# Two-layer hybrid encoder with a routed expert layer: expert weights read in 8 KB runs, and eight bias products spread over TensorE's row groups

## What is computed

```python
mod = cond @ ada_w[layer] + ada_b[layer]                 # 6 x 1024: shift, scale, gate, twice
h = _modulate(_rmsnorm(x, norm_mix_g[layer]), sh_m, sc_m)
m = mixer(h)              # layer 0: window attention + RG-LRU; layer 1: S5 state space + GLU
x = x + g_m * m
h = _modulate(_rmsnorm(x, norm_ffn_g[layer]), sh_f, sc_f)
x = x + g_f * _hier_moe(h, ...)
# _hier_moe: each token picks one of 4 groups, then the top 2 of its 4 experts;
#   for every expert e:  he = silu(t @ w1[e]) * (t @ w3[e]);  out += gate * (he @ w2[e])
#   w1, w3: [1024, 512], w2: [512, 1024], 16 experts in each layer
# GLU of layer 1: zg = act @ glu_w + glu_b;  zg[:, :1024] * sigmoid(zg[:, 1024:])
```

## Time and profile before

| | us |
|---|---|
| median of 3 runs | 899.51 (896.71 to 900.66) |
| the profiled execution | 902.16 |
| its span in the trace | 900.4 |
| PE (matmul) busy | 831.8 (92%) |
| VectorE, ScalarE, GpSimd busy | 316.3, 199.7, 146.9 |
| mean granted TensorE clock | 0.971 |
| DMA, mean over the span | 317 GB/s, 285.33 MB |

### The profile page before, as it was taken

One profiled execution on the slowest core, in us unless ns is written; L12 is line 12 of the kernel. 1 busy time (PEld: TensorE's weight loads), 2 busy tenths in 40 slices (PEclk: granted clock), 3 DMA queues, 4 the chain that ended last, 5 costly groups with the idle time before them and its releaser, 6 DMA issues.

```text
span 900.4 us, 12803 instructions
## 1 busy us (share of the span) xinstructions
PE 831.8 (92%) x5243; PEld 452.6 (50%) x5244; DVE 316.3 (35%) x718; ACT 199.7 (22%) x329; POOL 146.9 (16%) x234
## 2 busy tenths in 40 slices
PE   3899989899999998999599999689999899999994
PEld 0477634565564653644456544434444554655641
DVE  1447993741230411311799410621000311312304
ACT  2402330521311312312500110511001212213112
POOL 2328678049000000000033100000000000000000
PEclk9999989999999999999789999989999999999997
DMA  9999999969999999997996892206877399999992
GB/s 323 334 377 386 353 393 270 371 247 397 387 397 397 391 393 397 392 392 286 396 349 223 323 325 93 95 1 235 312 235 249 102 394 395 392 398 391 395 399 92
DMA packets 126289, 285.33 MB, mean 317 GB/s; under 512 B 7092, under 2 KB 8388, under 8 KB 125992
## 3 DMA queue, kind: packets, MB, share of 16 engines
q1 hardware_dynamic: 123552, 277.88, 84.1%
q0 software_dynamic: 1984, 5.21, 1.9%
q10 hardware_dynamic: 712, 1.67, 0.5%
HBM read 279.50 MB, written 5.24 MB: 316 GB/s over the span
## 4 chain that ended last, share of the span: by engine, by line
PE 71%; DMA 10%; DVE 8%; SPq 8%; issue 1%; ACT 1%; DVEq 0%; ACTq 0%
PE PS L1665 15%; PE PS L1684 11%; PE PS L1692 8%; DMA ring<-in_moe_w 7%; SPq L355 6%; PE PS L1971 6%; PE PS L1668 6%; PE PS L1708 6%; PE PS L1623 3%; PE PS L1434 3%; PE PS L1404 3%; DMA ring<-in_ab_w_in 2%; PE PS L1489 2%; PE PS L1956 2%; PE PS L1506 2%; SPq L364 2%
## 5 line engine op out<-in xcount | busy, mean ns | idle before, releaser
L1684 PE MATMUL PS<-ring,work 128*64 128x512 f32 (+1 forms) x512 | 129.0, 595 | 0.8 <-DMA ring<-in_moe_w 0.8
L1665 PE MATMUL PS<-ring,hT 128*64 128x256 f32 x896 | 107.6, 382 | 7.6 <-DMA ring<-in_moe_w 7.5
L1665 PE MATMUL PS<-ring,yg 128*64 128x256 f32 x896 | 106.2, 379 | 0.0
L1279 DVE TENSOR_TENSOR work<-work,PS 128x512 f32<-128x512 f32 x32 | 22.0, 688 | 207.9 <-PE PS L1665 159.6
L1665 PEld LDWEIGHTS PS<-ring,hT 128*64 128x64 f32 x896 | 61.9, 137 | 50.2 <-DMA ring<-in_moe_w 11.0
L1684 PEld LDWEIGHTS PS<-ring,work 128*64 128x64 f32 (+1 forms) x512 | 42.7, 143 | 76.1 <-issue 70.8
L1665 PEld LDWEIGHTS PS<-ring,yg 128*64 128x64 f32 x896 | 64.4, 137 | 32.3
L1692 PE MATMUL PS<-work,xhat 128*128 128x256 f32 (+1 forms) x256 | 68.1, 426 | 7.5 <-issue 7.2
L1283 DVE COPY yg<-PS 128x512 f32<-128x512 f32 x32 | 22.1, 692 | 146.3 <-PE PS L1684 146.3
L1708 PE MATMUL PS<-yg,grow 64*128 64x512 f32 (+1 forms) x256 | 68.0, 606 | 0.0
L1692 PEld LDWEIGHTS PS<-work,xhat 128*128 128x128 f32 x256 | 50.1, 198 | 28.2 <-issue 21.9
(11 more groups left out here) (366 smaller groups left out, 974.9 us busy)
## 6 DMA issues: line engine op xcount, KB each, us to landing
ring<-in_moe_w SPq DMA_DIRECT2D x96, 2048.0 KB, 19.2
ring<-in_ada_w SPq DMA_DIRECT2D x20, 2048.0 KB, 15.9
work<-in_ada_w SPq DMA_DIRECT2D x4, 2048.0 KB, 14.4
ring<-in_s_glu_w SPq DMA_DIRECT2D x4, 2048.0 KB, 17.2
ring<-in_ab_w_in SPq DMA_DIRECT2D x3, 2048.0 KB, 25.3
ring<-in_ab_w_out SPq DMA_DIRECT2D x2, 2048.0 KB, 14.8
ring<-rot_tables SPq DMA_DIRECT2D x2, 2048.0 KB, 10.6
rot_tables<-grow POOLq DMA_DIRECT2D x8, 256.0 KB, 5.8
```

What stands on the lines that cost most here:

```text
L1279: v.tensor_tensor(he[:, e % 2, :], he[:, e % 2, :], bank[1], ALU.mult).then_inc(S("he_ready"), 1)
L1665: last = mm(dst[64 * u:64 * u + 64, 0:256], hg[k][:, e * P:e * P + 64], w[:, k, 256 * u:256 * u + 256], start=k == 0, stop=k == KD - 1)
L1684: last = mm(dst, left[:, at:at + (64 if narrow else P)], w[:, c4, h * HALF:(h + 1) * HALF], start=c4 == 0, stop=c4 == KF - 1)
```

## The change

Three things change.

1. The expert weights are laid out so that one partition holds four consecutive rows of w1 and w3 (two of w2) in HBM: `"l e (h p c) f -> l p e h (c f)"`. A run is then 8 KB for all three. The contraction index k = 4h + c now stands for the model columns h*512 + p*4 + c. So everything that meets these weights has to have the columns in that order: `norm` writes `xhat` of the expert layers through `quads` (a read with a stride of four elements, a contiguous write), silu and the gated product go through `pairs` (a read of PSUM with a stride of two), and scale and shift of the expert layers come from new columns `mod4` and `gain4`, filled by 4 more transposes (`row4`), three more copies on ScalarE, and in `ada_cols(1)` and `ada_cols(2)` four more small products each, with one more addition on VectorE. The router weights are loaded in that order too, by 8 instead of 4 transfers on GpSimd's queue. ScalarE's queue issues four transfers for `row4` and drops two for the old rows.
2. `glub` stands four times, on partitions 0, 32, 64 and 96. Its transfers move from ScalarE's queue (one) to GpSimd's (four), behind the wait `x_new >= 2`.
3. `glu_bias(m, part, q)` uses row group q. The two of pair 0 stand in row groups 0 and 1; the two of pair 1 are issued together in the last turn of the loop; the four of pairs 2 and 3 are issued together at m == 2. The wait for `grow_ready >= 3` moves there from m == 3.

```diff
-        w1_v = a["moe_w1"].rearrange("l e (k p) f -> l p e k f", p=P)
-        w3_v = a["moe_w3"].rearrange("l e (k p) f -> l p e k f", p=P)
-        w2_v = a["moe_w2"].rearrange("l e (k p) n -> l p e k n", p=P)
+        w1_v = a["moe_w1"].rearrange("l e (h p c) f -> l p e h (c f)", h=2, c=4)
+        w3_v = a["moe_w3"].rearrange("l e (h p c) f -> l p e h (c f)", h=2, c=4)
+        w2_v = a["moe_w2"].rearrange("l e (u p c) n -> l p e u (c n)", u=2, c=2)
...
-                sp_.dma_start(u3(MOE_BASE[L] + j, D if w == "w2" else FF), moe_src(L, w, group * EPG + e)).then_inc(
+                sp_.dma_start(u3(MOE_BASE[L] + j, SLOT // 2), moe_src(L, w, group * EPG + e)).then_inc(
...
+        quads = lambda ap: ap.rearrange("q (h p c) -> q h c p", h=2, c=4)
+        quads_out = lambda ap: ap.rearrange("q (h c p) -> q h c p", h=2, c=4)
+        pairs = lambda ap: ap.rearrange("q (u p c) -> q u c p", u=2, c=2)
+        pairs_out = lambda ap: ap.rearrange("q (u c p) -> q u c p", u=2, c=2)
...
-                    s.activation(xhat[:, 0, :], x[:, 0, :], ACT.Copy, scale=stat[:, 6:7]).then_inc(S("xhat0_ready"), 1)
+                    src, dst = x[:, 0, :], xhat[:, 0, :]
+                    if n % 2:
+                        src, dst = quads(src), quads_out(dst)
+                    s.activation(dst, src, ACT.Copy, scale=stat[:, 6:7]).then_inc(S("xhat0_ready"), 1)
...
-                        s.activation(he[:, e % 2, :], bank[0], ACT.Silu).then_inc(S("sil_ready"), 1)
+                        s.activation(pairs_out(he[:, e % 2, :]), pairs(bank[0]), ACT.Silu).then_inc(S("sil_ready"), 1)
...
-                        v.tensor_tensor(he[:, e % 2, :], he[:, e % 2, :], bank[1], ALU.mult).then_inc(S("he_ready"), 1)
+                        v.tensor_tensor(pairs_out(he[:, e % 2, :]), pairs_out(he[:, e % 2, :]), pairs(bank[1]), ALU.mult).then_inc(S("he_ready"), 1)
...
                 dve.wait_ge(S("ada_cols_ps"), i + 1)
+                if i:
+                    dve.wait_ge(S("cols_ready"), 2)
+                    m4 = by_c(mod4[:, i - 1, :, :].rearrange("p s k -> p (s k)"))
+                    v.tensor_tensor(m4, bank[7][:, P:P + 16].rearrange("p (c m) -> p c m", c=4), m4, ALU.add)
...
                     last = mm(bank[6 if i == 0 else 7][:, c4 * n:(c4 + 1) * n], arows[i][:, c4 * P:(c4 + 1) * P],
                               sel[:, r:r + n], start=True, stop=True)
+                if i:
+                    f = r + 2
+                    for c in range(4):
+                        last = mm(bank[7][:, P + 4 * c:P + 4 * c + 4], arows[i][:, c::4], sel[:, f:f + 4], start=True,
+                                  stop=True)
...
+            for c in range(4):
+                tr(bank[5][:, P + 12 * c:P + 12 * c + 12], row4[:, c::4], 12)
...
+            pool.wait_ge(S("x_new"), 2)
+            for q in range(4):
+                pool.dma_start(glub[q], a["s5_glu_b"][0].rearrange("(r n) -> r n", r=4)).then_inc(S("glub_in"), 16)
...
-            def glu_bias(m, part):
+            def glu_bias(m, part, q):
-                r = GLU_PAIRS[m][0] + 2 * part
-                mm(bank[GLU_BANK[m][part]], bcol(ident[0:4, r:r + 1]), glub, start=True, stop=False)
+                r = 32 * q + GLU_PAIRS[m][0] + 2 * part
+                mm(bank[GLU_BANK[m][part]], bcol(ident[32 * q:32 * q + 4, r:r + 1]), glub[q], start=True, stop=False)
...
-                    glu_bias(0, 0)
-                    glu_bias(0, 1)
+                    glu_bias(0, 0, 0)
+                    glu_bias(0, 1, 1)
...
-                    glu_bias(1, 0)
+                    glu_bias(1, 0, 0)
+                    glu_bias(1, 1, 1)
                     glu_blocks(1, 0, 0, 3)
...
             for m in range(1, 4):
-                if m == 3:
+                if m == 2:
                     pe.wait_ge(S("grow_ready"), 3)
+                    for q in range(4):
+                        glu_bias(2 + q // 2, q % 2, q)
                 for part in range(1 if m == 1 else 0, 2):
-                    glu_bias(m, part)
                     glu_blocks(m, part, 0, KD)
```

More of the change, by code:

```diff
@@ L77 @@
 _at = 0
-for _name, _n in (("mix0", KD), ("ffn0", KD), ("mix1", KD), ("ffn1", KD), ("s5d", KD),
+for _name, _n in (("mix0", KD), ("mix1", KD), ("s5d", KD),
                   ("conv_w", CONV * LT), ("conv_b", LT), ("ga_b", LT), ("gx_b", LT), ("lam", LT)):
@@ L272, in build @@
         actT = yg[:, 2:4, :].rearrange("p a (k t) -> p (a k) t", t=T)
-        glub = yg[0:4, 1, HALF:D]
+        glub = [yg[32 * q:32 * q + 4, 1, HALF:D] for q in range(4)]
         arow1 = yg[:, 1, 0:HALF]
@@ L479, in _ @@
             for L in range(2):
[L480 to L483, removed]
+                for h in range(2):
+                    at = slice(4 * h, 4 * h + 4)
+                    rows4 = slice(h * HALF, (h + 1) * HALF)
+                    pool.dma_start(wr_sb[:, L, at, 0:NG], a["moe_wg"][L, rows4].rearrange(
+                        "(p c) g -> p c g", c=4)).then_inc(S("small_in"), 16)
+                    pool.dma_start(wr_sb[:, L, at, NG:], a["moe_we"][L, rows4].rearrange(
+                        "(p c) g e -> p c (g e)", c=4)).then_inc(S("small_in"), 16)
                 pool.dma_start(rb[:, L, 0:NG], a["moe_bg"][L:L + 1].to_broadcast([P, NG])).then_inc(S("small_in"), 16)
@@ L657, in modulate @@
                     act.wait_ge(S("xT_ps"), 4 * n + k // 2 + 1)
-                    s.activation(hT[:, k, :], bank[k // 2][:, (k % 2) * T:(k % 2 + 1) * T], ACT.Identity, scale=modA[:, n, k:k + 1],
-                                 bias=mod[:, L, sec, k:k + 1]).then_inc(S("hT_act"), 1)
+                    scale, shift = scaling(n, k)
+                    s.activation(hT[:, k, :], bank[k // 2][:, (k % 2) * T:(k % 2 + 1) * T], ACT.Identity, scale=scale,
+                                 bias=shift).then_inc(S("hT_act"), 1)
             def gate_row(n):
@@ L675, in _ @@
                 S("cols_ready"), 1)
+            row4_t = bank[5][:, P:P + 48].rearrange("p (c n) -> p c n", c=4)
+            s.activation(by_c(mod4[:, :, :, :].rearrange("p l s k -> p (l s k)")), row4_t[:, :, 0:8], ACT.Copy)
+            for L in range(2):
+                last = s.activation(by_c(gain4[L]), row4_t[:, :, 8 + 2 * L:10 + 2 * L], ACT.Copy)
+            last.then_inc(S("cols_ready"), 1)
             def rows_out(i):
@@ L798, in hg_evac @@
                 def hg_evac(k, at):
-                    return s.activation(hg[k], bank[at], ACT.Identity, scale=modA[:, n, k:k + 1],
-                                        bias=mod[:, L, SH_F, k:k + 1])
+                    scale, shift = scaling(n, k)
+                    return s.activation(hg[k], bank[at], ACT.Identity, scale=scale, bias=shift)
                 pt = lambda m: pickT[:, 2 * m:2 * m + 2, :].rearrange("p e t -> p (e t)")
@@ L849, in ffn @@
                         act.wait_ge(S(f"over_used{L}"), SLOTS + 3 * e + 1)
-                        s.activation(he[:, 0, :], bank[0], ACT.Silu).then_inc(did, 1)
+                        s.activation(pairs_out(he[:, 0, :]), pairs(bank[0]), ACT.Silu).then_inc(did, 1)
                         act.wait_ge(pe_did, KD + 1 + e + 1)
@@ L953, in norm @@
                 if n < 4:
[L954 removed]
+                    src, dst = x[:, 1, :], xhat[:, 1, :]
+                    if n % 2:
+                        src, dst = quads(src), quads_out(dst)
+                    v.tensor_scalar(dst, src, stat[:, 7:8], None, ALU.mult).then_inc(S("xhat1_ready"), 1)
                 else:
@@ L974, in mod_scale @@
             def mod_scale(n):
[L975 to L978, removed]
+                L = n // 2
+                if n % 2:
+                    dst, src, gain = mod4[:, L, 1, :], mod4[:, L, 1, :], gain4[L]
+                else:
+                    at = ROWS[("mix0", "mix1")[L]][0]
+                    dst, src, gain = modA[:, L, :], mod[:, L, SC_M, :], cols[:, at:at + KD]
+                v.scalar_tensor_tensor(dst, src, 1.0, gain, ALU.add, ALU.mult).then_inc(S("modA_ready"), 1)
                 dve.wait_ge(S("modA_ready"), n + 1)
             def modulate(n):
-                L, sec = n // 2, (SH_M if n % 2 == 0 else SH_F)
                 for k in (2, 3, 6, 7):
                     dve.wait_ge(S("xT_ps"), 4 * n + k // 2 + 1)
-                    v.tensor_scalar(hT[:, k, :], bank[k // 2][:, (k % 2) * T:(k % 2 + 1) * T], modA[:, n, k:k + 1],
-                                    mod[:, L, sec, k:k + 1], ALU.mult, ALU.add).then_inc(S("hT_dve"), 1)
+                    scale, shift = scaling(n, k)
+                    v.tensor_scalar(hT[:, k, :], bank[k // 2][:, (k % 2) * T:(k % 2 + 1) * T], scale, shift, ALU.mult,
+                                    ALU.add).then_inc(S("hT_dve"), 1)
             mod_evac(0)
```

36 lines of the change are left out of this document (23 added, 13 removed).

## The result

The changed kernel takes 893.93 us (median of 5 executions, 893.07 to 894.74), the kernel before 899.51 in the same comparison: ratio 0.9944, 95% interval [0.9924, 0.9963], 5.0 us less (3.3 to 6.8). A second comparison gave 891.9 us and 0.9898 [0.9876, 0.9920], 9.2 us less. These two intervals don't overlap, so ratios from different comparisons can be off by more than their own intervals say; a difference of about half a per cent between kernels of different comparisons shows no order, and what one gains on another is read from their stages. The two profiled executions, 902.16 before and 893.93 after, differ by 8.23 us, between the two. All three fall short of the 13.3 us that were forecast.

What follows compares the result with a forecast made beforehand. PE and the weight transfers were almost level, PE stalling on transfers in the expert layers. -7.9 - 2.7 - 4.7 + 1.6 + 0.4 = -13.3 us on 899.51 gave 886.2; range 883 to 889 (chance 0.62), wide range 881 to 895.

Steps and rivals of the forecast that it cites:

- biases that don't overlap: Rival: bias products in different row groups run one after the other, so their 4.7 us gain is lost: 891 us, chance 0.12.
- a ring that stays the bound: Rival: weight transfers still limit expert layer 0, at 5.21 to 5.40 us a unit; 890 us at 5.30, chance 0.10.
- the additional products: Four more small products each in `ada_cols(1)` and `ada_cols(2)`: +0.8 us each time, at most double.
- the norm: Expert layers' strided `norm`: +0.4 us for both on VectorE, bounds 0 to 1.2; ScalarE's half done earlier, costing nothing.
- the clock: Sign of being wrong: granted clock falling in a stage where it was granted in full; no term in the sum.
- The ring: Expert weight transfers in 8 KB runs, 5.05 us a unit: PE's stalls end, -7.9 us in layer 0, -2.7 in layer 1.
- Its thresholds: Unit times needed to end PE's stalls: 5.21 us in layer 0, 5.32 in layer 1; 4 KB runs' 5.19 below both.
- no effect: Rival: run length changes nothing, units stay at 5.40 us; only biases and additions count, -2.7 us: 897 us, chance 0.08.
- slower addresses: Rival: 8 KB runs lying farther apart in HBM slow the transfers; 918 us at 5.7 us a unit, chance 0.08.
- The biases: `glu_bias` products in row groups: three sets of 1.1, 1.1 and 1.3 us instead of 8.21, -4.7 us, bounds 0 to -5.5.

Runs made afterwards that it cites:

- e4: The changed kernel with w1 and w3 in runs of 4 KB, w2 left at 8 KB: 888.72 us, ratio 0.9873.
- e10: The kernel of e4 with w2 back at 4 KB runs in its old order: 888.3 us, ratio 0.9870.
- e5: The kernel before with four unread extra products in each of `ada_cols(1)` and `ada_cols(2)`, stationary operand in order: 902.73 us, beside 900.17 for the kernel before.
- e6: The kernel before with the same unread extra products as e5, stationary operand at every fourth column: 904.78 us, beside 900.17 for the kernel before.
- e12: The changed kernel with ScalarE writing the adaLN rows from PSUM a second time, reordered for the eight additional products: 886.38 us, ratio 0.9849.
- e8: The changed kernel measured once more, unedited, with a second profile: 891.9 us, ratio 0.9898 to the kernel before.

## Why the forecast was off

The measured 893.93 us lie within the wide range of the prediction, 881 to 895, but that is luck: its upper end was put there for biases that don't overlap or a ring that stays the bound, and neither happened. Two terms were mis-sized, the additional products and the norm, and one was missing, the clock.

**The ring: right in mechanism and size.** The groups came out at 59.3 us each and the layer at 237.1, and a unit at 4.97 us where 5.05 was taken, which had a loss of 1.5% in it that these stretches don't show. Its thresholds held too: 4 KB was said to suffice with 5.19 us against 5.21, and `e4` gives the same 237.01 us, `e10` 0.25 more. The two rules of the Trainium skill, "DMA: Bandwidth & Descriptors", that the prediction weighed are both contradicted. A fixed cost for each packet (section "Why small descriptors are slow (HBM only)") gave an estimate of 5.26 us a unit and a gain of 5.8 us in layer 0; measured were 4.97 and 7.95. Against line rate from 512 bytes on (section "Specifications") stand 387, 408 and 422 GB/s at runs of 2, 4 and 8 KB. The rivals of a ring in between, of no effect and of slower addresses are out with it.

**The biases: right, a little under.** Three sets of 1.06, 1.06 and 1.07 us; 1.1, 1.1 and 1.3 had been worked out. Four in four row groups cost what one costs. What the forecast left out is that the product sets beside a bias become shorter by 0.15 to 0.2 us each. Whether VectorE takes the 0.85 us of the pair in the loop back can't be told: the loop takes 76.5 to 77.8 us with the old biases and 75.6 to 77.1 with the new. That they don't overlap, the first rival, is out.

**Failed: the price of the additional products, "If the strided stationary operand costs nothing less or more, this stands; at most I allow double."** The measured value, 1.86 us, lies just beyond that double, 1.6. The products were priced by a row in which PE loads its stationary operand in order, and the stride was put at nothing. In order they cost 0.89 us (`e5`), with the stride 0.97 more (`e6`), and the weight load took 328 ns instead of 191. That the load sets the time is argued: the moving operand has only 4 columns, and 8 loads that are 0.137 us longer are 1.1 us, close to the 0.97. Sum over both places: +3.7, not +1.6.

**Failed: the norm, "ScalarE's half is done earlier and waits for nothing of this."** It is true of the kernel before, where VectorE's half is in the chain. But ScalarE's half also got the stride, grew from 1.15 to 2.15 us, and ScalarE's square root for rows 128 to 255 is queued behind it (line 675), so that VectorE's half starts later as well. In `e12` both stand in the chain one after the other, 2.13 and 1.17 us. The stage grew by 0.97 us in `e8` and `e12`, and by 1.73 in the kernel after, where the 16 transposes behind it took 3.63 us in one piece: the granted clock was 0.69 in 168 to 172 there, and 1.00 before. `e8` has no such fall, so it does not come with every execution of the kernel. In layer 1, of 1.06 us at most 0.4 is the stride's: the 4 KB kernels need 9.56 and 9.60 us there, the kernel after 9.96. The rest goes along with the clock: its mean was 0.81 in 563 to 572 before and 0.68 in 556 to 566 after, and the stage took 8.9 to 9.5 us in kernels with the old biases, 9.6 to 10.0 in those with the new. Nothing was tried on it, so that cause stays open. VectorE's own price, 0.76 to 1.17 us, lies inside the bounds that were given. The conditions of the Trainium skill, "VectorE: DVE Perf Modes", section "What auto-detection actually checks", name no step for float32; the prediction's reading, that the stride would then cost nothing, is contradicted at 16 bytes and agrees at 8 (0.77 us). Another page of the Trainium skill has a rule that fits: "SBUF — State Buffer", section "Door 1: The DMA port swizzle (why `[64,N]` ≈ `[32,N]`)", says that SBUF is read in lines of 16 bytes and needs two accesses to a line for full speed. A step of two floats has them, a step of four does not, and VectorE (0.77 and 1.17 us), ScalarE (1.24 and 2.15) and the weight load (196 and 328 ns) all agree. The same passage gives 4 float32 as how far one can stride for free; a step of four was not free here.

**Not foreseen: the clock.** The prediction's "if the clock fell in a stage where it is now granted in full" stood among the things that would make it wrong, and the sum had no term for it. It fell, and cost 1.70 us. Shown is that it comes with the products at every fourth column and the row-group biases together, and with neither alone. Why the two together bring it about stays open: no experiment varied what PE does between 501.91 and 515 any further.

Worked out from the table: the products 2.1 us, the norm and what follows it 2.4 (of its 2.8 in all, 0.97 in layer 0 and at most 0.4 in layer 1 are the stride's), the clock 1.7, less 1.1 for the biases, are the 5.1 us between -13.3 and -8.2. That is the account of two profiled executions; the medians of the two comparisons, -5.0 and -9.2, were not taken apart.

## What to carry to other kernels

A layout that speeds up transfers hands its permutation on to every reader, so price each reader on its own engine, those off the path too: what is queued behind them may be on it. Before the longest run is taken, ask which unit time the bound needs; here 4 KB was enough, and its step of 8 bytes was free where the 16 bytes of 8 KB nearly doubled an operation of ScalarE. If the long run is wanted, let a copy out of PSUM do the reordering: that took ScalarE 0.6 us a time beside other work, and the ratio to the kernel before fell from 0.9898 to 0.9849 (891.9 and 886.4 us, in two comparisons), with 2.67 us of it found in its stage.

## What was new about the hardware

- A stride of 16 bytes in SBUF: ScalarE 1.15 to 2.15 us for 128x1024 floats, VectorE 0.76 to 1.17, TensorE's weight load 191 to 328 ns. A stride of 8 bytes: 1.24, 0.77, 196 ns. In PSUM, a stride of 8 bytes left silu at 598 ns and the gated product at 688, and one of 16 bytes left ScalarE's copy of 512 floats at 0.60 us.
- Transfers of 2 MB ran at 387, 408 to 410, and 421 to 424 GB/s with runs of 2, 4 and 8 KB.
- Four 4-row products of 512 columns in four row groups took 1.07 us, one alone 1.05.
- In one profiled execution a VectorE copy within SBUF took 8.87 us beside GpSimd's work, and 0.62 without.
- TensorE's granted clock fell to a mean of 0.57 to 0.59 over 4 us, that is to 1.2 GHz for some 3.4 us, without an idle gap ahead, in the three profiled executions with both the products at every fourth column and the row-group biases, and in none of the eleven others.
